# Twelve homes instead of four for the weight tiles of the opening, eight of them in the second half of a work tile

## The chip, the cores and the metric

The kernel is one program on one core of a Trainium2 chip. The core has five engines with instruction streams of their own: TensorE (PE; its weight loads are listed apart as PEld), VectorE (DVE), ScalarE (ACT), GpSimd (POOL) and SyncE (SP), which here only starts transfers. Sixteen DMA engines move data between device memory (HBM) and the on-chip buffer (SBUF). The metric is device time of the whole program in microseconds (us), the median of several runs.

## The reference, cut to what matters

The program is a small transformer on 256 tokens (and 256 context tokens) of width 2048, all in float32: two layers that project, attend and project back, then a mixing block and a gated feed-forward block. What matters here is how the first layer begins:

```
sc, scc = silu(c), silu(c_ctx)
shift, scale, gate       = split(sc  @ w_ada[0] + b_ada[0], 3)     # 2048 x 6144
shift_c, scale_c, gate_c = split(scc @ w_ada[0] + b_ada[0], 3)
h  = rms(x,  norm_w[0]) * (1 + scale)   + shift
hc = rms(xc, norm_w[0]) * (1 + scale_c) + shift_c
u  = h @ w_in[0]          # its columns z (the gate of the output) are computed first
```

So before the first projection can run, two thirds of the first layer's `w_ada` (shift and scale) has to be multiplied with two vectors, and the mean of the squares of x has to be known.

## The kernel before, in words

All weights are cut into tiles of 128 x 1024 float32 (512 KB) and packed by the host in the order of use, as one stream. A planner (`make_plan`) writes the program as a list of steps, and every engine walks the same list and emits its part, so each engine's order is fixed. SP walks the list of loads: it waits until the tile's home (its buffer) is free and starts the transfer. `place_loads` gives out the homes in turn: `RAW` = 4 homes in the buffer `raw` during the opening and most of the program, three more for a while in each layer's attention (`pl.more`: from load a to load b these homes join the turn).

A tile of `w_ada` ("ada chunk", L698) is read by TensorE straight from its home: two k-tiles of 128 rows, against a stationary operand of 32 columns. It is free again once TensorE has done it (semaphore `ada_used`). Eight chunks (group g, c = 0 to 7) make one row of 512 outputs. ScalarE copies the row out (L988, `ada_row`), TensorE turns it into columns (L705, `ada_turn`), VectorE adds the bias (L1342).

A tile of a projection is split: ScalarE copies it rounded into `whi` (L982), VectorE writes the rest into `wlo` (L1332), and the home is free after that (semaphore `lo`). TensorE then does three passes per product (L788 to L790), 24 matmuls of 512 columns per tile in the first projection group, z0 ("z chunk" below).

The opening interleaves these: groups 0 to 7 of `w_ada` (64 chunks), the squares of x (ScalarE squares one of 16 tiles at L994 and L1001, GpSimd adds it to the sum at L1761), their mean (L712, L720), the tiles of h (VectorE L1373, ScalarE L1020 and L1025, VectorE L1384), and five z chunks, one after every few ada chunks. Loads 0 to 70 carry the 64 ada chunks and z chunks 0 to 6. The mean stands in TensorE's order behind ada chunk 2.2 (load 20), z chunk 0 behind chunk 3.1 (load 27), and the last turn (`ada_turn` 7) behind chunk 7.7 (load 70). x itself (4 MB), the constants and the rope table come through GpSimd's queue (q0), everything of SP through q1. GpSimd prepares the rope table (L1770, L1774) ahead of its first sum.

The work tile `T` has 32 rows of 512 numbers per partition. x lies in rows 0 to 15. Rows 16 to 31 are first written when the queries, keys and latents of layer 0 are made, which comes after all of z.

Of the kernel before, what the change touches and what calls it, by code (L numbers as in the profile page):

```python
# [33 lines left out]

CH = 1024
RAW = 4
RAW_ATT = 3
RING = 3
LEAD = 2
# [128 lines left out]
def tail_groups():  # L168
    def span(a):
        return [(a, a + 512)]  # L170

    mix, ffn = [], []
    for g in range(4):
        mix.append(Group("u", None, g, DT, 512, span(512 * g), L + WINDOWS[g], "hn", 4, "w_in_2", "hn_mix" if g == 0 else None))
    for j in range(4):
        mix.append(Group("gc", None, j, DT, 512, span(2 * D + 512 * j), L + 2, "hn", 1, "w_in_2"))
        if j == 0:
            for g in range(4):
                mix.append(Group("ya", None, g, 4, 512, [(0, 512)], L, "pooled", 1, "pool_w_2", "pooled"))
        mix.append(Group("v", None, j, DT, 512, span(3 * D + 512 * j), L + 2, "hn", 1, "w_in_2"))  # L180
        mix.append(Group("gb", None, j, DT, 512, span(D + 512 * j), L, "latent", 4, "w_in_2"))
    for j in range(4):
        mix.append(Group("ga", None, j, DT, 512, span(4 * D + 512 * j), L, "latent", 4, "w_in_2"))
        mix.append(Group("gbr", None, j, DT, 512, span(5 * D + 512 * j), L, "latent", 1, "w_in_2"))
        mix.append(Group("mix", None, j, DT, 512, span(512 * j), L, "conv", 4, "conv_out_w_2",
                         "conv" if j == 0 else None))
    for j in range(4):
        mix.append(Group("wo", None, j, DT, 512, span(512 * j), L, "mixed", 4, "w_o_2", "mixed" if j == 0 else None))
    for g in range(FT // 2):
        ffn.append(Group("ffn", None, g, DT, 512, [(256 * g, 256 * g + 256), (FFN + 256 * g, FFN + 256 * g + 256)], L,  # L190
                         "hn", 2, "w_gate_up_2", "hn_ffn" if g == 0 else None))
    for j in range(4):
        ffn.append(Group("down", None, j, FT, 512, span(512 * j), L, "ffn", 4, "w_down_2", "ffn" if j == 0 else None))
    return mix, ffn
# [15 lines left out]
def slots_of(l):  # L210
    streams = 1 if l else 2
    places = [(u, c, q) for u in range(len(UNITS)) for c in range(streams) for q in range(2)]
    return [Slot(l, s, u, c, q, streams) for s, (u, c, q) in enumerate(places)]
# [7 lines left out]
class Plan:  # L221
# [69 lines left out]
    def place_loads(self):  # L291

        turn, last = list(range(RAW)), {}
        for n in range(len(self.loads)):
# [21 lines left out]
def make_plan():  # L316
    pl = Plan()
    every = []
    layers = [layer_groups(l) for l in range(DEPTH)]
    mix, ffn = tail_groups()  # L320
    for first, second, third in layers:
        every += first + second + third
    every += mix + ffn
    pl.enqueue(every)

    pl.add("start")
    opening = layers[0][0]
    chunks = pl.chunks(opening, DT)
    for i in range(ADA_FIRST):
        for c in range(8):  # L330
            pl.ada(i, c)
            if c == 7:
                pl.add("ada_row", i)
            if i < 2:
                pl.add("square", "x", 8 * i + c)
            if i == 1 and c in (2, 6):
                pl.split()
            if i == 2 and c == 2:
                pl.add("mean", "x")
                pl.add("layer", 0)  # L340
            if c == 3 and i:
                pl.add("ada_turn", i - 1)
                if i % 2 == 0:
                    pl.add("scale", 0, i // 2 - 1)
            if c >= 4 and i and i % 2 == 0:
                pl.add("make", opening[0], 2 * i - 4 + c - 4)
            if i % 2 and i > 1 and (c == 1 or c == 5 and i < 7):
                next(chunks)
    pl.add("ada_turn", ADA_FIRST - 1)
    pl.add("scale", 0, 3)  # L350
    for k in range(12, DT):
        pl.add("make", opening[0], k)
    for _ in chunks:
        pass
    nada, full = [ADA_FIRST * 8], []

    def ada_turn():
        if full:
            pl.add("ada_turn", full.pop())

    def ada_some(n):
        for _ in range(n):
            g, c = divmod(nada[0], 8)
            pl.ada(g, c)
            nada[0] += 1
            if c == 7 and g != ADA_BETWEEN:
                pl.add("ada_row", g)
                full.append(g)

    for l, (first, second, third) in enumerate(layers):  # L370
        if l:
            pl.add("layer", l)
            ada_some(4)
            pl.add("scale", l, None)
            chunks = pl.chunks(first)
            next(chunks)
            pl.add("ada_row", ADA_BETWEEN)
            next(chunks)
            pl.add("ada_turn", ADA_BETWEEN)
            for _ in chunks:  # L380
                pass
        pl.add("rq", l)
        pl.gemm(second)
        pl.flush()
        pl.add("barrier", ("gemm", l))
        pl.left[l] = pl.owner
        pl.turn, pl.owner = 0, {0: None, 4: None}
        slots = slots_of(l)
        att_from = len(pl.loads)
        for s in range(len(slots)):  # L390
            pl.add("score", l, slots, s)
            ada_turn()
            if s < len(ADA_PACE[l]):
                ada_some(ADA_PACE[l][s])
            pl.add("att", l, slots, s)
            if s >= len(slots) - 3:
                pl.add("make", third[0], s - len(slots) + 3)
        more = RAW + RAW_ATT * l
        pl.more.append((att_from, len(pl.loads), list(range(more, more + RAW_ATT))))
        chunks = pl.chunks(third, 3)  # L400
        for s in range(len(slots), len(slots) + 4):
            pl.add("att", l, slots, s)
            next(chunks)
        pl.add("attended", l, slots)
        for _ in chunks:
            pass
        if l == 0:
            for n, p in zip((2, 1, 1, 0), pl.pending):
                pl.add("evac", *p)
                ada_some(n)  # L410
            pl.pending = []
        pl.flush()
    pl.add("tail")
    pl.gemm(mix)
    pl.flush()
    pl.add("ffn")
    pl.gemm(ffn)
    pl.flush()
    pl.add("final")
    pl.place_loads()  # L420
    return pl


def build(nc, d):
    pl = make_plan()
    S = {}

# [5 lines left out]
    hi, lo, used, ada_used = sig("hi"), sig("lo"), sig("used"), sig("ada_used")  # L433
# [41 lines left out]
    place[0] += (WEIGHTS_AT - place[0]) % 256  # L475
    raw = own("raw", [P, RAW, CH])
    whi = own("whi", [P, RING, CH], F32R)
# [14 lines left out]
    T = sb("T", [P, 32, 512], F32, t_at)  # L492
# [106 lines left out]
    def raw_of(n):  # L599

        h = pl.homes[n]
        if h < RAW:
            return raw[:, h, :]
        l, i = divmod(h - RAW, RAW_ATT)
        if i < 2:
            return LF[:, 12 + 2 * i:14 + 2 * i, :].rearrange("p a b -> p (a b)")
        return wlo_f[:, idle_split[l] % RING, :]
# [12 lines left out]
    keys_last = [next(g for g in pl.groups if g.kind == "wkvb" and g.layer == l and g.index == 2) for l in range(DEPTH)]  # L620
# [38 lines left out]
    def sync_engine(SP):  # L659
        SP.dma_start(param[:, :], d["param"]).then_inc(*param_in.up("in"))  # L660
        for n, what in enumerate(pl.loads):
            h = pl.homes[n]
            if pl.before[n] is not None:
                was = pl.loads[pl.before[n]]
                if was[0] == "ada":
                    SP.wait_ge(*ada_used.at(was[1], was[2]))
                else:
                    SP.wait_ge(*lo.at(was[0].id, was[1]))
            elif h >= RAW:
                SP.wait_ge(*used.at("done", keys_last[(h - RAW) // RAW_ATT].id))  # L670
            width = CH
            if what[0] != "ada":
                g, c = what
                width = min(g.kpc, g.kt - c * g.kpc) * g.width
            SP.dma_start(raw_of(n)[:, 0:width], d["stream"][n][:, 0:width]).then_inc(*raw_in[h].up(n))
        for j in range(4):
            SP.wait_ge(*v_ev.at("final", j))
            SP.dma_start(d["out"][:, 4 * j:4 * j + 4, :], SCALED[:, 4 * j:4 * j + 4, :]).then_inc(*out_out[j].up("out"))
        for j in range(4):
            SP.wait_ge(*out_out[j].at("out"))  # L680
# [1378 lines left out]
```

## Time and profile before

| | us |
|---|---|
| median of 3 runs | 3344.04 |
| the three runs | 3344.04, 3333.69, 3369.77 |
| the profiled execution | 3341.04 |
| its span | 3339.7 |
| TensorE busy in the span | 3221.7 (96%) |

The page divides the span into 40 slices of 83.5 us. Its first two slices are the opening and the only ones, beside those around the attention of layer 0, in which TensorE waits much. Windows of the trace give the same for shorter stretches: busy time of each engine, the clock that was granted to TensorE as a share of 2.4 GHz, how busy the 16 DMA engines were and what they moved. The waits say which instruction waited for what, and the timeline says when. Matmul ends are modelled, so the start of the next instruction is the better mark.

### The profile page before, as it was taken

The numbers are of one execution on the slowest core, as the hardware profiler recorded it, in microseconds if no ns is written. First come the engines' busy times: TensorE is split into PE (matmuls) and PEld (weight loads), VectorE is DVE, ScalarE is ACT, GpSimd is POOL, SyncE is SP. The second block draws the span as 40 slices with busy tenths as digits, with TensorE's granted clock in tenths as the row PEclk, the third lists the DMA queues.
The fourth block names the chain that finished last, engine by engine and source line by source line (L and its number), as shares of the span: only waits on it lengthen the run. The fifth ranks groups of instructions, "written<-read, shape, count | busy, mean of one in ns | idle before, by whom it ended". The sixth has DMA issues, their size and how long they took to land.

```text
span 3339.7 us, 52153 instructions
## 1 busy us (share of the span) xinstructions
PE 3221.7 (96%) x21958; PEld 2798.5 (84%) x21958; DVE 1670.4 (50%) x2688; ACT 1360.4 (41%) x2179; POOL 173.5 (5%) x252
## 2 busy tenths in 40 slices
PE   6899999988999999999899999999999999999998
PEld 2488888873558879887559999999999999999998
DVE  1322233376763354354775675556555655555454
ACT  2322232344542254334454443334444444444443
POOL 3001000001001101000111000000000000000000
PEclk9899999998999989999999999999999999999999
DMA  8633222226754246433425455555555555555554
GB/s 305 252 124 123 95 95 95 79 84 252 268 181 153 96 186 209 145 128 106 168 82 197 156 183 184 188 187 192 195 192 195 171 195 194 193 195 194 192 195 158
DMA packets 152826, 566.09 MB, mean 170 GB/s; under 512 B 17520, under 2 KB 17648, under 8 KB 151440
## 3 DMA queue, kind: packets, MB, share of 16 engines
q1 hardware_dynamic: 146160, 529.52, 45.4%
q0 software_dynamic: 6432, 33.23, 2.8%
q8 instruction: 173, 2.83, 0.3%
q14 instruction: 61, 0.50, 0.0%
HBM read 550.10 MB, written 12.58 MB: 168 GB/s over the span
## 4 chain that ended last, share of the span: by engine, by line
PE 91%; DVE 3%; DMA 3%; issue 1%; ACT 1%; POOL 1%; SPq 0%; DVEq 0%; POOLq 0%; ACTq 0%
PE ps L788 20%; PE ps L790 20%; PE ps L789 20%; PE ps L777 7%; PE ps L779 7%; PE ps L778 7%; PE ps L698 3%; DMA sb_raw<-in_stream 2%; PE ps L910 2%; PE ps L873 1%; PE ps L896 1%; PE ps L864 1%; PE ps L889 1%; PE ps L705 1%; DMA sb_rope<-in_rope 1%
## 5 line engine op out<-in xcount | busy, mean ns | idle before, releaser
L1332 DVE TENSOR_TENSOR sb_wlo<-sb_raw,sb_whi 128x1024 fp32r<-128x1024 f32 (+1 forms) x814 | 992.5, 1220 | 1311.2 <-ACT sb_whi L982 1310.0
L982 ACT ACTIVATE sb_whi<-sb_raw 128x1024 fp32r<-128x1024 f32 (+1 forms) x818 | 860.1, 1053 | 1084.1 <-PE ps L790 839.2
L788 PE MATMUL ps<-sb_hn_hi,sb_whi 128*128 128x256 f32 (+4 forms) x2944 | 821.9, 279 | 4.8 <-DVE sb_hn_lo L1404 4.1
L789 PE MATMUL ps<-sb_hn_lo,sb_whi 128*128 128x256 f32 (+4 forms) x2944 | 820.9, 279 | 0.0
L790 PE MATMUL ps<-sb_hn_hi,sb_wlo 128*128 128x256 f32 (+4 forms) x2944 | 820.4, 279 | 0.0
L788 PEld LDWEIGHTS ps<-sb_hn_hi,sb_whi 128*128 128x128 f32 x2944 | 555.6, 189 | 5.6 <-DVE sb_hn_lo L1404 4.4
L790 PEld LDWEIGHTS ps<-sb_hn_hi,sb_wlo 128*128 128x128 f32 x2944 | 556.0, 189 | 0.0
L789 PEld LDWEIGHTS ps<-sb_hn_lo,sb_whi 128*128 128x128 f32 x2944 | 555.6, 189 | 0.0
L779 PE MATMUL ps<-sb_whi,sb_lo 128*128 128x512 f32 (+1 forms) x968 | 375.0, 387 | 0.0
L777 PE MATMUL ps<-sb_whi,sb_hi 128*128 128x512 f32 x896 | 354.8, 396 | 0.0
L778 PE MATMUL ps<-sb_wlo,sb_hi 128*128 128x512 f32 x896 | 349.0, 390 | 0.0
L788 PE MATMUL ps<-sb_hi,sb_whi 128*128 128x512 f32 (+1 forms) x1024 | 343.4, 335 | 0.0
L789 PE MATMUL ps<-sb_lo,sb_whi 128*128 128x512 f32 (+1 forms) x1024 | 341.8, 334 | 0.0
L790 PE MATMUL ps<-sb_hi,sb_wlo 128*128 128x512 f32 (+1 forms) x1024 | 341.8, 334 | 0.0
L788 PEld LDWEIGHTS ps<-sb_hi,sb_whi 128*128 128x128 f32 x1024 | 192.2, 188 | 25.7 <-issue 5.8
L779 PEld LDWEIGHTS ps<-sb_whi,sb_lo 128*128 128x128 f32 x968 | 182.0, 188 | 36.6
L790 PEld LDWEIGHTS ps<-sb_hi,sb_wlo 128*128 128x128 f32 x1024 | 193.3, 189 | 20.0
L789 PEld LDWEIGHTS ps<-sb_lo,sb_whi 128*128 128x128 f32 x1024 | 192.3, 188 | 19.7
L777 PEld LDWEIGHTS ps<-sb_whi,sb_hi 128*128 128x128 f32 x896 | 168.6, 188 | 35.4 <-DVE sb_scr L1373 1.7
L778 PEld LDWEIGHTS ps<-sb_wlo,sb_hi 128*128 128x128 f32 x896 | 168.5, 188 | 34.8
L790 PE MATMUL ps<-sb_ffn_hi,sb_wlo 128*128 128x256 f32 x704 | 194.3, 276 | 0.0
L788 PE MATMUL ps<-sb_ffn_hi,sb_whi 128*128 128x256 f32 x704 | 194.3, 276 | 0.0
(269 smaller groups left out, 4040.5 us busy)
## 6 DMA issues: line engine op xcount, KB each, us to landing
sb_raw<-in_stream SPq DMA_DIRECT2D x943, 512.0 KB, 3.4
sb_lo_f<-in_stream SPq DMA_DIRECT2D x33, 512.0 KB, 6.0
sb_wlo_f<-in_stream SPq DMA_DIRECT2D x16, 512.0 KB, 5.8
sb_raw<-in_stream SPq DMA_DIRECT2D x18, 384.0 KB, 2.9
sb_T<-in_x POOLq DMA_DIRECT2D x1, 4096.0 KB, 18.1
z_scratch<-sb_scr POOLq DMA_DIRECT2D x16, 256.0 KB, 2.6
sb_zb<-z_scratch POOLq DMA_DIRECT2D x16, 256.0 KB, 2.9
sb_bias<-in_bias POOLq DMA_DIRECT2D x4, 1024.0 KB, 8.3
```

The lines of the kernel that those rows point to most:

```text
L698: mm = PE.matmul(PS[t:t + 32, ada_bank(g), :], cond[:, k, :], raw_of(n)[:, 512 * j:512 * j + 512], start=k < 4, stop=k >= 12, tile_positio ...
L705: mm = PE.matmul(PS[:, ada_bank(g), 2 * m:2 * m + 2], arow_of(g)[:, m * P:(m + 1) * P], C("sum4"), start=True, stop=True)
L777: PE.matmul(o, xh[:, xt], wh, start=k == 0, stop=False)
L778: PE.matmul(o, xh[:, xt], wl, start=False, stop=False)
L779: mm = PE.matmul(o, xl[:, xt], wh, start=False, stop=k == g.kt - 1)
L788: PE.matmul(o, whi[:, s, w], xh, start=k == 0, stop=False)
L789: PE.matmul(o, whi[:, s, w], xl, start=False, stop=False)
L790: mm = PE.matmul(o, wlo[:, s, w], xh, start=False, stop=k == g.kt - 1)
L864: PE.matmul(out[h], T[:, T_QN + head, qs], key_nope(head)[:, ks], start=True, stop=True, skip_group_check=True)
L910: mm = PE.transpose(PS[:, 4 + h, kt * P:kt * P + P], p_of(t, h)[:, kt * P:kt * P + P], ident)
L982: AC.activation(whi[:, s, 0:width], raw_of(n)[:, 0:width], ACT.Copy).then_inc(*hi.up((g.id, c)))
L1332: VE.tensor_tensor(wlo[:, s, 0:width], raw_of(n)[:, 0:width], whi[:, s, 0:width].bitcast(F32), ALU.subtract).then_inc(*lo.up((g.id, c)))
```

## The change

The opening's loads get twelve homes: the four of `raw`, and eight in rows 16 to 31 of `T`, two rows each. They join the turn from load 0 up to the load that the planner has reached when the opening's loop ends (load 71, not included). After that four homes are left, as before. The order of the loads, the steps and all computation stay as they are. The homes of the attention stages get other numbers, nothing else.

```diff
+RAW_OPEN = 8
...
             if i % 2 and i > 1 and (c == 1 or c == 5 and i < 7):
                 next(chunks)
+    pl.more.append((0, len(pl.loads), list(range(RAW, RAW + RAW_OPEN))))
...
-        more = RAW + RAW_ATT * l
+        more = (RAW + RAW_OPEN) + RAW_ATT * l
...
         if h < RAW:
             return raw[:, h, :]
-        l, i = divmod(h - RAW, RAW_ATT)
+        if h < RAW + RAW_OPEN:
+            a = 16 + 2 * (h - RAW)
+            return T[:, a:a + 2, :].rearrange("p a b -> p (a b)")
+        l, i = divmod(h - (RAW + RAW_OPEN), RAW_ATT)
...
-            elif h >= RAW:
-                SP.wait_ge(*used.at("done", keys_last[(h - RAW) // RAW_ATT].id))
+            elif h >= (RAW + RAW_OPEN):
+                SP.wait_ge(*used.at("done", keys_last[(h - (RAW + RAW_OPEN)) // RAW_ATT].id))
```

SP's order of loads at the start of the program, before (`ada_used` is TensorE's release of a home, `lo` VectorE's):

```order
L660 DMA sb_param<-in_param 128x364 [waits barrier_Pool_Activation_PE_DVE_SP_release]
L675 DMA sb_raw<-in_stream 128x1024 x4
L675 DMA sb_raw<-in_stream 128x1024 [waits ada_used] x11
L675 DMA sb_raw<-in_stream 128x1024 [waits lo]
L675 DMA sb_raw<-in_stream 128x1024 [waits ada_used] x4
L675 DMA sb_raw<-in_stream 128x1024 [waits lo]
```

and with the change:

```order
L665 DMA sb_param<-in_param 128x364 [waits barrier_Pool_Activation_PE_DVE_SP_release]
L680 DMA sb_raw<-in_stream 128x1024 x4
L680 DMA sb_T<-in_stream 128x1024 x8
L680 DMA sb_raw<-in_stream 128x1024 [waits ada_used] x4
L680 DMA sb_T<-in_stream 128x1024 [waits ada_used] x7
L680 DMA sb_T<-in_stream 128x1024 [waits lo]
```

Before, the fifth load waits for a release; now the thirteenth is the first that does. Load 15 waited for the split of z chunk 0 (load 11); now load 23 does.

ScalarE's order in the same place, before (the squares are L1001, the splits L982, the copy of a row L988):

```order
L1001 ACTIVATE sb_scr<-sb_T 128x512 [waits p_ev] x4
L988 ACTIVATE sb_scr<-ps 128x512 [waits ada_used]
L1001 ACTIVATE sb_scr<-sb_T 128x512 [waits p_ev] x4
L982 ACTIVATE sb_whi<-sb_raw 128x1024 [waits raw_in3]
L1001 ACTIVATE sb_scr<-sb_T 128x512 [waits p_ev] x4
L982 ACTIVATE sb_whi<-sb_raw 128x1024 [waits raw_in0]
L988 ACTIVATE sb_scr<-ps 128x512 [waits e_ev,ada_used]
```

and with the change:

```order
L1006 ACTIVATE sb_scr<-sb_T 128x512 [waits p_ev] x4
L993 ACTIVATE sb_scr<-ps 128x512 [waits ada_used]
L1006 ACTIVATE sb_scr<-sb_T 128x512 [waits p_ev] x4
L987 ACTIVATE sb_whi<-sb_T 128x1024 [waits raw_in11]
L1006 ACTIVATE sb_scr<-sb_T 128x512 [waits p_ev] x4
L987 ACTIVATE sb_whi<-sb_T 128x1024 [waits raw_in4]
L993 ACTIVATE sb_scr<-ps 128x512 [waits e_ev,ada_used]
```

The order is the same. The two splits and the row copies stand between the squares as they did, and wait for tiles that have other homes.

## Rows read from the trace of the kernel before

**Rows 1.** The page: TensorE's busy tenths in 40 slices of the span.

```profile
PE   6899999988999999999899999999999999999998
```

**Rows 2.** Windows: us, busy time by engine, granted clock, DMA share, GB/s.

```profile
0.00:10.00 10.00, 1.92 (x4) 0.19 (x4) 0.66 (x9) 1.52 (x2) 2.48 (x8) 1.00 0.85 318
10.00:15.00 5.00, 0.00 (x0) 0.00 (x0) 0.00 (x0) 0.00 (x0) 0.00 (x0) 1.00 1.04 445
15.00:20.00 5.00, 1.92 (x4) 0.19 (x4) 0.00 (x0) 0.00 (x0) 0.00 (x0) 1.00 0.90 375
20.00:22.70 2.70, 1.92 (x4) 0.19 (x4) 0.00 (x0) 1.67 (x3) 0.00 (x0) 1.00 1.04 423
...
56.00:147.00 91.00, 77.80 (x360) 36.57 (x359) 27.10 (x61) 26.59 (x48) 0.00 (x0) 0.87 0.80 294
147.00:160.00 13.00, 13.00 (x61) 10.89 (x62) 8.83 (x18) 8.72 (x15) 0.00 (x0) 1.00 0.29 96
```

**Rows 3.** Waits of SP, 0 to 160 us: total us, times, longest.

```profile
SPq L675 <- PE ps L698: 97.3, 49, 11.1
SPq L675 <- DVE sb_wlo L1332: 32.9, 9, 11.3
```

**Rows 4.** Timeline, 16 to 60 us: start, length, what, idle before.

```profile
16.07 1.92 PE L698 MATMUL ps<-sb_raw,sb_cond 128*32 128x512 f32 x4 [9.52 <-DMA sb_raw<-in_stream]
20.20 0.63 ACT L994 ACTIVATE sb_scr<-sb_T 128x512 f32<-128x512 f32 x1 [16.78 <-DMA sb_T<-in_x]
22.83 2.48 POOL L1770 TENSOR_TENSOR sb_rope<-sb_rope,sb_const 128x512 f32<-128x512 f32 x2 [19.77 <-DMA sb_rope<-in_rope]
27.26 20.38 POOL L1761 TENSOR_TENSOR sb_scr<-sb_scr 128x512 f32<-128x512 f32 x14
45.74 1.92 PE L698 MATMUL ps<-sb_raw,sb_cond 128*32 128x512 f32 x4 [4.53 <-DMA sb_raw<-in_stream]
52.50 1.26 POOL L1761 TENSOR_TENSOR sb_scr<-sb_scr 128x512 f32<-128x512 f32 x1 [4.85 <-ACT sb_scr L1001]
55.17 1.05 PE L712 MATMUL ps<-sb_const,sb_scr 128*128 128x1 f32 x8
57.88 1.05 PE L698 MATMUL ps<-sb_raw,sb_cond 128*32 128x512 f32 x4
```

**Rows 5.** DMA of 14 to 17 us by queue: packets, MB, share.

```profile
q0 software_dynamic: 35, 1.08, 83.4%
q1 hardware_dynamic: 40, 0.14, 11.4%
```

**Rows 6.** Timeline, 60 to 105 us: tiles of h, z chunk 0, ada chunks, turns.

```profile
63.08 0.69 DVE L1384 TENSOR_TENSOR sb_lo<-sb_scr,sb_hi 128x512 fp32r<-128x512 f32 x1 [0.84 <-ACT sb_hi L1025]
67.80 0.50 PE L788 MATMUL ps<-sb_hi,sb_whi 128*128 128x512 f32 x1
73.47 1.06 PE L698 MATMUL ps<-sb_raw,sb_cond 128*32 128x512 f32 x8
74.46 1.05 PE L705 MATMUL ps<-sb_const,sb_scr 128*128 128x2 f32 x8
75.44 1.06 PE L698 MATMUL ps<-sb_raw,sb_cond 128*32 128x512 f32 x8
90.02 1.92 PE L698 MATMUL ps<-sb_raw,sb_cond 128*32 128x512 f32 x4 [2.43 <-DMA sb_raw<-in_stream]
93.67 3.64 PE L698 MATMUL ps<-sb_raw,sb_cond 128*32 128x512 f32 x16
```

**Rows 7.** Timeline, 146 to 148 us: the last row and turn.

```profile
146.29 0.60 ACT L988 ACTIVATE sb_scr<-ps 128x512 f32<-128x512 f32 x1 [11.37 <-PE ps L698]
146.94 1.05 PE L705 MATMUL ps<-sb_const,sb_scr 128*128 128x2 f32 x8 [0.69 <-ACT sb_scr L988]
```

**Rows 8.** Windows with several loads queued; the second in layer 0's attention.

```profile
33.00:38.00 5.00, 3.03 (x15) 0.57 (x11) 0.00 (x0) 2.79 (x5) 4.57 (x4) 1.00 0.99 333
770.00:780.00 10.00, 5.66 (x36) 1.10 (x24) 5.08 (x18) 6.53 (x19) 0.12 (x1) 0.84 0.98 371
```

## The prediction

> **What bounds the kernel now.** I read the page's slices first: TensorE is busy in nine tenths or more of nearly every slice, and the first is an exception, at six tenths [rows 1]. The change touches loads 0 to 70, so I cut the opening into windows. From 56 to 147 us TensorE is busy 77.8 of 91.0 us at a mean granted clock of 0.87, and the DMA engines are at 0.80 and move 294 GB/s; in the 13 us behind it TensorE is busy throughout at clock 1.00 and the DMA engines at 0.29 [rows 2]. So the opening is short of weights until its last turn starts at 146.94 us [rows 7], and from there TensorE is the bound. The waits of SP say why the weights are late: of the opening it spends 97.3 us waiting for TensorE to release a home and 32.9 us for VectorE to finish a split [rows 3]. Loads are issued late while the engines that carry them have room. What is won ahead of 146.94 us is kept whole, because nothing behind it waits for an absolute time.
>
> **The first part: up to the mean.** Nothing of the computation changes. The sixteen squares need x and GpSimd. x is in at 20.20 us, and GpSimd starts on the rope table at 22.83, sums from 27.26 on, and has done 14 sums in 20.38 us [rows 4], 1.41 us each with one gap. The fifteenth sum starts only at 52.50, after 4.85 us of waiting for ScalarE, whose square stands behind a split and a row copy that wait for late tiles. The mean follows at 55.17 behind ada chunks that are late too [rows 4]. With the tiles early, the fifteenth sum ends at 27.26 + 15 x 1.41 = 48.4; the two splits and the row copies still stand between the squares, for which I add 1.1. Call it 49.5 us.
>
> Are the tiles early? By 22.7 us the windows give 3.18 + 2.23 + 1.88 + 1.14 = 8.4 MB [rows 2]. 5.5 MB of that are x, constants, parameters and rope table, so 2.9 MB or 5.6 tiles of 0.524 MB are weights. For the pitch behind it the trace has stretches in which several loads are queued: 371 GB/s at share 0.98 with seven homes in the attention, 333 at 0.99 with four homes here [rows 8], and 423 at the end of the table's load [rows 2]. That is 1.41, 1.57 and 1.24 us per tile. I take 1.38, nearest to the row with the most homes, and keep 1.24 and 1.57 as ends. Load n then lands at 22.7 + (n + 1 - 5.6) x 1.38: load 20, the last ahead of the mean, at 44, before the sums are done. The mean starts at 49.5 instead of 55.2. This is worth **5.7 us**.
>
> Does x come later, with twelve weight loads beside it instead of four? From 14 to 17 us q0 moved 1.08 MB and q1 0.14 [rows 5], though loads 1 to 3 were queued on q1 at that time (TensorE got the first of them only at 16.07 us [rows 4]). x had nearly nine tenths of the bytes against a waiting weight queue. A longer queue waits just as much; I cost this at 0, with a rival below.
>
> **The second part: from the mean to the last turn.** Before it is 146.94 - 55.17 = 91.8 us. TensorE's own work in it, at the full level of its clock:
> - mean and rows until ada chunk 2.3: 57.88 - 55.17 = 2.7 [rows 4];
> - 45 ada chunks. Two that lie ready take 74.46 - 73.47 = 0.99 together [rows 6], while one that arrives alone takes 0.98 or more. 45 x 0.49 = 22.1;
> - 6 turns x (75.44 - 74.46) = 5.9 [rows 6];
> - 5 z chunks x (73.47 - 67.80) = 28.3 [rows 6];
> - row copy ahead of the last turn 146.94 - 146.29 = 0.7 [rows 7].
>
> Sum 59.7 us. Three more terms:
> - Tiles of h. The first is ready 3.9 us behind turn 1's end (63.77 against 59.85) [rows 6]. TensorE needs about 3 us for the six ada chunks between. So z chunks 0, 2 and 4, the first of each pair of fresh tiles, wait 0.3, 1.0 and 0.9: 2.2 us.
> - The clock. TensorE stands still from 45 to 49.5. In this trace the wait of 4.5 us ahead of 45.74 is followed by chunks of 1.92 us, and the one of 2.4 us ahead of 90.02 too; at 93.67 four chunks take 3.64 instead of 2.0 [rows 4, 6]. The mean clock of 0.87 [rows 2] is what such stretches leave; they last 8 to 12 us. I let everything from the mean to z chunk 0 run at the 1.2 GHz level. This costs 6.7 us: a second time the mean and rows (1.9), the lone chunk 2.3 (1.4), the turn (0.8) and six chunks (2.6).
> - DMA. z chunk 0 starts at 63.5. Until then TensorE has released all homes up to load 27, so SP has issued up to 39, and load 39 lands at 70: the queue does not run dry by more than 1 us. Load 45 lands at 78, needed at 85. Load 63 lands at 103, needed at 107. Load 70 lands at 113, needed at 117. Each is early, so 0. At 1.57 us load 70 lands at 125.4.
>
> Last turn: 49.5 + 59.7 + 2.2 + 6.7 = **118.1 us**, against 146.94: 28.8 earlier. For further falls of the clock, of which the stretch before has three and each costs up to 4 us when TensorE is the bound, I take back 2. From load 71 on four homes are back; their last users (ada chunks 6.6 to 7.1) are long done, and a z chunk needs a tile in 5.7 us, so the stage behind is as before: 0. The attention homes have new numbers only: 0. Eight more semaphores: 0.
>
> Sum: 3341.0 - 28.8 + 2 = 3314.2 against the profiled execution. The median of the runs shown is 3.0 above it, and I give the result as **3316**.
>
> The Trainium skill, "DMA: Bandwidth & Descriptors", Specifications, puts the HBM limit of one core at about 358 GB/s, which speaks against more homes being of full use. By it, as an estimate, a tile takes 1.46 us, load 70 lands at 118 and the last turn starts near 121, 3 us later than in my sum. The trace exceeds it in short windows and is near it in the long one.
>
> **The rivals.**
> 1. *The stream is slower than I take it* (as at 33 to 38 us, 333 GB/s at share 0.99 [rows 8]). Load 70 lands at 125.4, the turn starts at about 128, and the gain is 19: 3325. For it: this row is of this very stage. Against it: it has four homes, and 371 comes with seven. Chance 0.17.
> 2. *More than 1%.* No fall of the clock while TensorE waits for the mean, and 1.24 us per tile. The turn starts at 118.1 - 6.2 = 112, as z chunk 0 is then held by its tile of h. The gain is 35: 3309 or less. For it: the windows at 423 and 445 GB/s [rows 2]. Against it: 4.5 us of waiting brought the low clock before. Chance 0.18.
> 3. *x comes later.* If q0 and q1 share evenly, x and rope table (5.3 MB) need twice their bytes at 0.38 MB/us, until about 28.6 us instead of 22.8, and the mean starts at 55.3. The rest is TensorE's and follows: gain 23, 3321. Chance 0.06.
> 4. *Slower: x starves behind twelve queued tiles.* The place is q0 in the first 30 us. If x got a fifth of the bytes, it and the table would take 5.3 / 0.076 = 70 us, the mean would start at 97, and the last turn at 165: 18 us later, 3362. It decides from a mean at 79 us on (147 less the 68 that follow it). Rows 5 speak against it. The chance of a result that is slower is 0.03, and over 1% slower (33 us) needs x later still: 0.01.
> 5. *The change does nothing*, because the sums and tiles of h are the chain anyway: 3344. Against it: the ladder above leaves that chain 28 us of room. Chance 0.04.
>
> My forecast, a gain of 23 to 33 us by the sum above, has 0.52.
>
> **How the numbers follow.** The low end is rival 2's (3309) less 5 for the scatter of the runs (3334 to 3370), 3304. The high end is rival 1's with 10 for the scatter above, 3336. One per cent is 33 us, about what a measurement of this kernel tells from no change. Faster by over 1% is rival 2 and a little scatter, 0.20; slower by over 1% 0.01 and scatter, 0.02; within it 0.78.
>
> The Trainium skill, "TensorE: Matmul & The Clock Gate", HAM oscillation, says that matmul groups which wait for their data fall back to the half clock each time, so feeding them early gives back more than the waits. By that rule the mean clock from 56 us to the last turn should rise above the 0.87 of rows 2; I have it rise, but for the one fall at the mean.
>
> **What would show it.** SP's waits for L698 shift by eight loads, and twelve loads stand open. x lands at 20 to 21 us. The mean starts at 49 to 51. The waits of L698 for tiles behind it are below 5 us in all. The last turn starts at 116 to 122. DMA moves 340 to 400 GB/s from 23 to 60 us. Behind the last turn all stages have their old lengths. I am wrong if x lands after 25 us, if DMA stays below 330 GB/s with loads queued, or if a stage behind grows by what the opening lost.

## The result

The changed kernel takes 3313.09 us (median of 4 runs, 3312.15 to 3315.54), the kernel before 3343.49 (4 runs, 3333.69 to 3369.77). The ratio is 0.989 with a 95% interval from 0.984 to 0.993, so it is faster by about 1.1%. Forecast were 3316 us and a range from 3304 to 3336. The span of the profiled execution fell from 3339.7 to 3310.8 us.

The windows of the changed kernel, cut as in [rows 2] but with the long one behind 56 us ending at 118 us, 2 us behind its own last turn (columns: window and length; busy time of PE, PEld, DVE, ACT, POOL; granted clock; DMA share; GB/s):

```profile
20.00:22.70 2.70, 1.94 (x6) 0.18 (x4) 0.00 (x0) 1.67 (x3) 0.00 (x0) 1.00 1.03 419
22.70:30.00 7.30, 6.21 (x24) 0.99 (x24) 0.00 (x0) 0.63 (x1) 6.56 (x6) 1.00 1.02 410
30.00:40.00 10.00, 8.04 (x34) 2.49 (x32) 0.00 (x0) 5.59 (x9) 9.00 (x8) 0.79 1.03 410
40.00:50.00 10.00, 5.13 (x18) 0.65 (x16) 4.57 (x4) 5.89 (x9) 9.14 (x7) 0.84 1.02 409
50.00:60.00 10.00, 9.26 (x52) 5.40 (x52) 3.01 (x10) 1.18 (x4) 0.12 (x1) 0.68 1.01 392
56.00:118.00 62.00, 58.53 (x359) 34.54 (x358) 26.94 (x65) 26.03 (x47) 0.00 (x0) 1.00 0.95 371
118.00:131.00 13.00, 13.00 (x59) 10.76 (x58) 9.16 (x15) 8.91 (x15) 0.00 (x0) 1.00 0.23 67
```

From 20 to 50 us the DMA engines are full and carry 409 to 419 GB/s. From 56 us on they carry 371 where they carried 294 before, and TensorE is busy 58.5 of 62 us at clock 1.00, where it was 77.8 of 91 at 0.87.

The timeline of the same execution at the places of [rows 4] and [rows 7] (start, length, instruction, idle time before it):

```profile
20.41 0.63 ACT L999 ACTIVATE sb_scr<-sb_T 128x512 f32<-128x512 f32 x1 [16.85 <-DMA sb_T<-in_x]
23.05 2.49 POOL L1775 TENSOR_TENSOR sb_rope<-sb_rope,sb_const 128x512 f32<-128x512 f32 x2 [19.98 <-DMA sb_rope<-in_rope]
27.49 22.64 POOL L1766 TENSOR_TENSOR sb_scr<-sb_scr 128x512 f32<-128x512 f32 x15
50.17 1.87 PE L717 MATMUL ps<-sb_const,sb_scr 128*128 128x1 f32 x8 [4.42 <-POOL sb_scr L1766]
54.62 1.89 PE L703 MATMUL ps<-sb_T,sb_cond 128*32 128x512 f32 x4
56.44 1.05 PE L710 MATMUL ps<-sb_const,sb_scr 128*128 128x2 f32 x8
...
115.94 1.05 PE L710 MATMUL ps<-sb_const,sb_scr 128*128 128x2 f32 x8 [0.74 <-ACT sb_scr L993]
```

x is in 0.2 us later than before. GpSimd now does its 15 sums without a long stop, and TensorE waits for them, no longer for tiles. The mean starts at 50.17 us instead of 55.17, the last turn at 115.94 instead of 146.94: 31.0 us, of which 5.0 lie ahead of the mean and 26.0 behind it.

Less than half of the 26.0 us is time in which TensorE stood still for a tile. These are the ada chunks from the mean to the last turn (busy us, mean ns of one matmul, idle time before them), the first line of the kernel before, the others of the changed one:

```profile
L698 PE MATMUL ps<-sb_raw,sb_cond 128*32 128x512 f32 x182 | 41.9, 732 | 11.9 <-DMA sb_raw<-in_stream 11.9
```

```profile
L703 PE MATMUL ps<-sb_T,sb_cond 128*32 128x512 f32 x120 | 16.8, 615 | 0.0
L703 PE MATMUL ps<-sb_raw,sb_cond 128*32 128x512 f32 x60 | 9.0, 596 | 0.2 <-DMA sb_raw<-in_stream 0.2
```

The wait went from 11.9 to 0.2 us, and the same chunks took 25.8 us instead of 41.9. Both sides of that are in the prediction's rows: at the low level of the clock a lone chunk takes 1.92 us, and two that lie ready take 0.99 together at the full one, where a lone one takes nearly as much by itself [rows 4, 6]. How the 16 us divide between the two was not measured.

Behind the last turn the work is as it was. Two windows of equal length, the first of the kernel before from 1.1 us behind its last turn, the second of the changed one from 3.1 us behind its own:

```profile
148.00:3339.70 3191.70, 3115.27 (x21502) 2755.90 (x21502) 1639.10 (x2614) 1318.28 (x2108) 147.07 (x225) 0.98 0.47 163
```

```profile
119.00:3310.80 3191.80, 3116.13 (x21494) 2758.10 (x21492) 1637.57 (x2607) 1318.14 (x2107) 147.17 (x225) 0.98 0.48 163
```

From the last turn to the end of the span it was 3192.8 us before and is 3194.9 now, 2.1 us more. In nine of the twelve profiled executions of this document that stretch lies between 3190.4 and 3195.3, so the 2.1 us are no more than its scatter. Of the 31.0 us of the opening 28.9 arrived at the end. In the experiments below I compare the start of the last turn rather than spans, because the late stages scatter by more than some of these kernels differ (last section).

### The profile page after: what moved, and what is told of

Read it like the earlier page. It is cut to its first block, busy times and chain, and to the rows that moved or that the text cites. A ratio compares the mean times of both kernels' runs of the same rounds, so it can differ in the third digit from the quotient of the medians.

```text
span 3310.8 us, 52153 instructions
## 1 busy us (share of the span) xinstructions
PE 3206.1 (97%) x21958; PEld 2801.9 (85%) x21958; DVE 1671.6 (50%) x2688; ACT 1360.2 (41%) x2179; POOL 174.5 (5%) x252
## 4 chain that ended last, share of the span: by engine, by line
PE 92%; DVE 3%; DMA 2%; issue 1%; ACT 1%; POOL 1%; SPq 0%; POOLq 0%; DVEq 0%; ACTq 0%
PE ps L793 20%; PE ps L795 20%; PE ps L794 20%; PE ps L782 7%; PE ps L784 7%; PE ps L783 7%; PE ps L703 2%; PE ps L915 2%; PE ps L878 1%; PE ps L901 1%; DMA sb_raw<-in_stream 1%; PE ps L869 1%; PE ps L894 1%; PE ps L710 1%; POOL sb_scr L1766 1%
## 5 line engine op out<-in xcount | busy, mean ns | idle before, releaser
L987 ACT ACTIVATE sb_whi<-sb_raw 128x1024 fp32r<-128x1024 f32 x812 | 853.6, 1052 | 1068.6 <-PE ps L795 841.7
```

What stands on the lines that cost most here:

```text
L987: AC.activation(whi[:, s, 0:width], raw_of(n)[:, 0:width], ACT.Copy).then_inc(*hi.up((g.id, c)))
```

## The experiments

All are the changed kernel with one edit, but for e7. "Last turn" is the start of the eighth L710 (L705 in the kernels with four homes). The times are those of one profiled execution each. x landed between 18.97 and 20.41 us in them (29.14 in e6), and differences of 1 us in the table are within that scatter: the change and e8 are the same kernel. The last column comes from all runs of each.

| kernel | mean starts | last turn | between | ratio to before (95%) |
|---|---|---|---|---|
| four homes (before) | 55.17 | 146.94 | 91.8 | 1 |
| six, e5 | 51.59 | 129.81 | 78.2 | 0.993 (0.990 to 0.995) |
| eight, e3 | 49.83 | 121.67 | 71.8 | 0.994 (0.991 to 0.997) |
| twelve, the change | 50.17 | 115.94 | 65.8 | 0.989 (0.984 to 0.993) |
| twelve, e8 | 48.93 | 115.09 | 66.2 | 0.990 (0.987 to 0.992) |
| twelve from load 21 on, e1 | 54.21 | 122.03 | 67.8 | 0.993 (0.990 to 0.995) |
| twelve up to load 20, e2 | 48.70 | 143.41 | 94.7 | 1.000 (0.997 to 1.004) |
| twelve, x in 4 KB rows, e6 | 58.84 | 124.44 | 65.6 | 0.993 (0.990 to 0.997) |
| four, rope table later, e7 | 51.07 | 147.91 | 96.8 | 0.999 (0.996 to 1.002) |
| twelve, rope table later, e4 | 44.56 | 111.38 | 66.8 | 0.989 (0.985 to 0.993) |
| the same, e10 | 45.41 | 111.29 | 65.9 | 0.988 (0.984 to 0.992) |
| twelve, filler ahead of the mean, e9 | 49.57 | 114.49 | 64.9 | 0.992 (0.989 to 0.996) |

**Which part of the opening needs the homes.**

```diff
-    pl.more.append((0, len(pl.loads), list(range(RAW, RAW + RAW_OPEN))))
+    pl.more.append((21, len(pl.loads), list(range(RAW, RAW + RAW_OPEN))))    # e1
+    pl.more.append((0, 21, list(range(RAW, RAW + RAW_OPEN))))                # e2
```

> The eight extra homes join only at load 21, the first tile behind the mean; up to it four homes as before. My theory (two separate gains: about 5 us ahead of the mean, the rest because TensorE finds its tiles ready behind it): the mean starts at 55 us as in the kernel before, the DMA engines then run at about 400 GB/s, and the last turn starts at 118 to 121 us, 26 to 29 us ahead of the kernel before. Rival (the lead has to be built up while TensorE waits for the squares, so that late homes are worth little): last turn at 130 us or later.

> The extra homes are there for loads 0 to 20 only. My theory: the mean starts at 50 us as with the change, but behind it the stretch costs what it cost before (91 us, less 0 to 3 us), so the last turn starts at 139 to 142 us, 5 to 8 us ahead of the kernel before. Rival (the lead is what counts): last turn at 130 us or earlier.

Late homes alone start the last turn at 122.03, 24.9 us ahead of before (1 us later than I expected). Early homes alone give 3.5 us, less than expected, and no change of the time that can be measured. The windows show what the DMA engines did. First e1, then e2:

```profile
56.00:100.00 44.00, 42.27 (x233) 23.44 (x234) 18.90 (x41) 17.45 (x31) 0.00 (x0) 1.00 1.02 405
```

```profile
50.00:56.00 6.00, 5.43 (x27) 3.58 (x31) 0.87 (x3) 0.26 (x1) 0.00 (x0) 0.62 0.04 8
56.00:100.00 44.00, 35.65 (x162) 16.34 (x155) 16.83 (x37) 16.49 (x30) 0.00 (x0) 0.92 0.85 296
```

With late homes the DMA engines are full. In e2 they stand still from 50 to 56 us (share 0.04): the four homes are full while TensorE waits for the mean, and behind it the stream starts afresh at 296 GB/s. Between the mean and the last turn TensorE waited 14.8 us for tiles in e2 and 11.9 in the kernel before. The two parts do not add: the early one is worth 6.1 us beside the late one (122.03 - 115.94) and 3.5 without it.

**How many homes.**

```diff
-RAW_OPEN = 8
+RAW_OPEN = 4    # e3: eight homes
+RAW_OPEN = 2    # e5: six homes
```

> Eight homes instead of twelve (four of them in the work tile). By the count of loads that may stand open: the mean at 50 us as with the change; the bursts of ten and twelve ada chunks behind z chunks 1 and 3 outrun the queue by 1 to 2 us each. Last turn at 117 to 120 us, 27 to 30 us ahead of the kernel before. Rival (a tile in flight takes long with a long queue, so each home counts): halfway between four and twelve, about 131 us.

> Six homes (two of them in the work tile). From the mean to the last turn the stretch took 91.8 us with four homes, 71.8 with eight, 65.8 with twelve. My theory (what counts is whether the lead covers a burst of ten or twelve ada chunks): the first two homes bring more than the next two; mean at 51 to 52 us, then about 79 us, last turn at 128 to 133. Rival (linear in the homes between four and eight): 134 to 135 us.

Two more homes bring 17.1 us, the next two 8.1, the last four 5.7. e5 came out as expected. e3 is 1.7 us behind the expected range, but far from the rival's 131. From the mean to the last turn TensorE waited 11.9 us for tiles with four homes, 7.1 with six, 4.7 with eight (nearly all of it in the bursts of ten and twelve ada chunks) and 0.2 with twelve; what is left at twelve is TensorE's own work and 2.5 us of waiting for tiles of h.

**What protects x.** The change puts twelve tiles beside x.

```diff
-                PO.dma_start(T[:, 0:16, :], d["x"]).then_inc(*x_in.up("in"))
+                for k in range(0, 16, 2):
+                    PO.dma_start(T[:, k:k + 2, :], d["x"][:, k:k + 2, :]).then_inc(*x_in.up("in"))
```

> Twelve homes, and x comes as eight transfers with rows of 4 KB instead of one with rows of 32 KB. My theory (x had nearly nine tenths of the bytes because its pieces are eight times as long as those of the weights, and the length of the weight queue did not matter): both queues share evenly, x is in at 24 to 26 us and the rope table at 27 to 29 instead of 20.4 and 23.1, the mean starts at 55 us and the last turn at 119 to 122. Rival (a queue's turn does not depend on the size of its pieces): x at 20 to 21 us, last turn at 116. Rival (x waits for the twelve tiles): mean at 66 us or later.

The DMA queues from 14 to 17 us (packets, MB, share of the 16 engines), with the change, and in e6:

```profile
q0 software_dynamic: 34, 1.11, 86.5%
q1 hardware_dynamic: 33, 0.12, 9.7%
```

```profile
q1 hardware_dynamic: 173, 0.63, 52.1%
q0 software_dynamic: 171, 0.62, 51.2%
```

In both, the two queues move nearly equal numbers of packets: 34 and 33, 171 and 173 (with four homes 35 and 40 [rows 5]). What differs is the size. x's packets carried 33 KB each and the weights' 4 KB; in e6 all carry 4 KB. By this x keeps nine tenths of the bytes against twelve tiles (q0 had 1.08 MB against four [rows 5]) and falls to half when its rows are cut. x came in at 29.14 us in e6, the mean started at 58.84, both later than I expected (24 to 26, 55). The likely reason is that q0 carries the constants, x and the table, and shares from the first microsecond, which I had not counted; no run separates it. The last turn was 8.5 us later than with the change, nearly all of the mean's 8.7. The Trainium skill, "DMA: Bandwidth & Descriptors", Queues, rings and completion order, says that each DMA engine goes round its queues packet by packet; the counts of this trace agree.

**What bounds the mean.**

```diff
                 PO.wait_ge(*const_in.at("in"))
                 make_rope(0)          # taken out of the step "start", ahead of the sums
...
+            elif st[0] == "mean":     # and put behind them
+                PO.wait_ge(*const_in.at("in"))
+                make_rope(0)
```

> Twelve homes, and GpSimd prepares the rope table behind the sums of the squares instead of ahead of them. My theory (with twelve homes the mean is bound by GpSimd's sums, not by tiles): sums start at about 21 instead of 27.5 us, the mean at 44 to 45 us instead of 50.2, just behind load 20 at 42 to 43; the last turn at 109 to 111 us, where load 70 becomes the bound (22.7 + 65.4 x 1.28 = 106.4, and 3.5 behind it): 5 to 7 us less than with the change alone. Rival (the wait is hidden by the tiles of h or by the weight stream): no change, 116 us.

> e4 again with more rounds, beside a kernel with the same homes: last turn at 110 to 112 us, median 3303 to 3308, 0.987 to 0.989 of the kernel before.

> Four homes as before, and the rope table is prepared behind the sums. With twelve homes this brought 4.6 us. My theory (with four homes too the squares hold up the split of z chunk 0, and so home 3 and load 15): load 15 is issued 5 us earlier, the mean starts at 50 to 51 instead of 55.2, the last turn at 142 to 143. Rival (with four homes the tiles alone set the mean): 146 to 147 us, as before.

With twelve homes the mean moves from 50.2 to 44.6 and the last turn to 111.4, 4.6 us, a little less than expected. Counted from the landing of x, the mean came 29.7 us later in the change, e2, e3, e6, e8 and e9, and 25.3 in e4 and e10: in these kernels it follows GpSimd. The DMA engines are at 1.03 and 409 GB/s in e4 from 56 to 100 us, and in the longer bursts of ada chunks TensorE is paced by the tiles, one every 1.28 us:

```profile
56.00:100.00 44.00, 42.90 (x246) 23.57 (x244) 15.54 (x36) 15.42 (x28) 0.00 (x0) 1.00 1.03 409
```

```profile
74.48 1.05 PE L703 MATMUL ps<-sb_T,sb_cond 128*32 128x512 f32 x4 [0.23 <-DMA sb_T<-in_stream]
75.76 1.05 PE L703 MATMUL ps<-sb_T,sb_cond 128*32 128x512 f32 x4 [0.23 <-DMA sb_T<-in_stream]
77.04 1.05 PE L703 MATMUL ps<-sb_T,sb_cond 128*32 128x512 f32 x4 [0.23 <-DMA sb_T<-in_stream]
```

TensorE is busy 42.9 of 44 us in the same window, and its last four chunks find their tiles ready, so both are near their limit.

With four homes (e7) the same edit moves the mean by 4.1 us, as my theory said, and the last turn not at all (147.91, where I expected 142 to 143). The rival's number came out, though for another reason than its own: not the tiles ahead of the mean, but the stream behind it, for whose tiles TensorE then waited 16.4 us instead of 11.9. The median of e4 was 3304.95 us in 6 runs, that of e10 3311.57 in 11, above the expected 3303 to 3308. Ratios of 0.989 and 0.988 beside 0.989 and 0.990 for the change do not tell the version from it; the profiles do, by 4 us. By its last turn it is the earliest of these kernels.

**The clock at the mean.**

```diff
             elif st[0] == "mean":
+                PE.wait_ge(*const_in.at("in"))
+                for _ in range(4):
+                    PE.matmul(PS[:, 4, :], ident, const[:, 0:512], start=True, stop=True)
                 PE.wait_ge(*p_ev.at("sq", "x", DT - 1))
```

> Twelve homes, and between ada chunk 2.2 and the mean TensorE does four matmuls of constants into a bank that nothing uses yet (about 0.9 us each at the full clock), so that it stands still for 1 to 2 us there instead of 4.4. My theory (the 4.4 us of standing still bring the 1.2 GHz level, which costs 2.5 us from the mean to turn 1 and passes whole to the end): the mean at 50 to 51 us, from its start to turn 1 3.7 us instead of 6.3, last turn 2 to 3 us earlier, 113 to 114 us. Rival (the tiles of h or the weight stream bind behind it anyway, or the clock falls all the same): 115 to 117 us.

TensorE in e9 around the mean (L717):

```profile
45.10 3.70 PE L934 MATMUL ps<-sb_const 128*128 128x512 f32 x8
49.57 1.05 PE L717 MATMUL ps<-sb_const,sb_scr 128*128 128x1 f32 x8 [0.78 <-POOL sb_scr L1768]
51.19 1.16 PE L725 MATMUL ps<-sb_const,sb_ssq 128*128 128x128 f32 x8 [0.57 <-DVE sb_ssq L1357]
52.28 1.84 PE L703 MATMUL ps<-sb_T,sb_cond 128*32 128x512 f32 x4
54.05 1.87 PE L710 MATMUL ps<-sb_const,sb_scr 128*128 128x2 f32 x8
55.85 1.93 PE L703 MATMUL ps<-sb_T,sb_cond 128*32 128x512 f32 x8
```

The mean ran at the full level, but the low one came all the same, from 52.3 us on, with no wait over 0.8 us in the 7 us ahead of it. From the mean to turn 1 it took 4.5 us instead of 6.3, where I expected 3.7, and the last turn came at 114.49, 0.6 us ahead of e8 and 1.5 ahead of the change. x had landed at 19.84, 19.20 and 20.41 us in the three, so this shows no clear gain at the last turn. The theory that the wait of 4.4 us brings the low level does not hold as I put it. e10 has the same fall, from about 47.0 to 50.7 us, with a wait of 0.6 us.

Over all profiled executions, the five in which TensorE waited 1.8 us or more right ahead of the mean (the change, e2, e3, e6, e8) had the low level behind it and took 5.3 to 6.3 us from the mean to turn 1. Of the seven others, five took 3.7 us and two had the low level: e9 (4.5) and e10 (5.3, while e4, the same kernel, took 3.7). So the low level came with every such wait, but also twice without one. What brings it about there is open.

**The control.**

> The changed kernel again, on the chip and in the hour of these runs: last turn at 115 to 117 us, median 3311 to 3316.

Last turn 115.09, median 3311.06: as expected.

## Why the prediction was right, point by point

- **The bound, and that the gain is kept.** Right but for 2.1 us. Up to the last turn SP waited for TensorE 36.6 us instead of 97.3 [rows 3], and 28.9 of the 31.0 us arrived at the end. Its waits for VectorE hardly changed, 25.8 us after 20.9. SP's waits from 0 to 116 us:

```profile
SPq L680 <- PE ps L703: 36.6, 27, 5.4
SPq L680 <- DVE sb_wlo L1337: 25.8, 4, 9.2
```

- **The mean.** 49.5 forecast, 50.17 measured; 15 sums took 22.64 us, 1.51 each instead of 1.41 with 1.1 added, and x was 0.2 us late. The 1.41 is not what [rows 4] give over all 14 sums, which is 20.38 / 14 = 1.46; with that the forecast would have been 50.2. But the term of 5.7 us was put down as if it stood by itself. e2 and e7 show that with four homes behind the mean it is worth 3.5 us or nothing: the stream behind the mean takes it back.
- **x.** 0 was right, and e6 shows what it rests on. Rivals 3 and 4 fell.
- **The tile pitch.** This size was off: 1.38 us taken, 1.28 measured (0.524 MB at 410 GB/s), near the end of 1.24. The row nearest to the true value was that of the end of the table's load [rows 2]; the row at 770 us [rows 8], which I took as nearest because it has the most homes, was too slow. The error cost nothing, since with twelve homes TensorE binds; in e4, where tiles pace the longer bursts, the last turn came at 111.4, near the 109.9 that the new pitch gives. Rival 1 fell with it. The HBM limit of 358 GB/s that the Trainium skill gives ("DMA: Bandwidth & Descriptors", Specifications) did not hold here: 409 and 410 GB/s stood for 27 us.
- **From the mean to the last turn.** 68.6 us by my sum, 65.8 measured. The clock was mis-sized: I let everything up to z chunk 0 run at 1.2 GHz, at a cost of 6.7 us. The low level ended with chunk 2.3, and from the mean to turn 1 it took 6.3 us where the kernel before took 3.7, so the cost was 2.6 us. No further fall came: the mean granted clock was 1.00 from 56 to 118 us. So the 2 us taken back for further falls were not due; that the stretch behind the last turn took 2.1 us more made up for them by luck. That the wait at the mean is the cause of the low level, as the term supposed, is not shown: e9 had that level without a wait over 0.8 us. The tiles of h cost 2.5 us where I had 2.2, but with another division: z chunks 0 and 2 waited 1.3 and 1.2 us and z chunk 4 not at all, where I had 0.3, 1.0 and 0.9.
- **The queue not running dry.** Nearly: SP issued nothing from 61.5 to 67.9 us. Load 40 needs the home of load 28, whose split ScalarE starts only at 65.60 us, behind four tiles of h and a row copy; VectorE ends its part at 67.91. SP's timeline from 60 to 70 us:

```profile
59.84 1.65 SPq L680 DMA_DIRECT2D sb_raw<-in_stream  x3
67.93 1.28 SPq L680 DMA_DIRECT2D sb_T<-in_stream  x3
```

  The DMA share was 0.83 to 0.86 from 68 to 80 us behind it. I counted TensorE's releases only, and overlooked this one; the stock of tiles covered it.
- **Rival 2** (over 1%) had one of its two conditions, the pitch, and not the other. The ratio came out between it and the forecast: I gave 0.20 to a gain of over 1%, and the measured 1.1% has an interval from 0.7 to 1.6.
- **The sum and the signs.** The sum was 3314.2 us for the profiled execution, which took 3312.15. With the 3.0 us added for the median it makes 3317.2 and not the 3316 that I gave. Of the signs named, two were missed: the last turn came at 115.94, just ahead of 116 to 122, and DMA moved 409 and 410 GB/s from 23 to 50 us, above 340 to 400.

## What to carry to other kernels

In this kernel the homes had to cover the longest burst of chunks that are used up quickly, not the mean rate: four homes left the DMA engines at 0.80 while TensorE waited, and each pair more brought less (17, 8, then 3 us). Tiles that come early gave back more than the waits for them, since the chunks themselves took 16 us less. Memory that is written only later in the program is a free place for them. Before moving a producer earlier, ask what stands behind it: with four homes 4 us at the mean were worth nothing, with twelve 4.6.

## What the runs showed of the hardware

- Queues shared the DMA engines by packets, so the size of a transfer's rows set its share: 86.5% of the engines' time with 32 KB rows, 51.2% with 4 KB rows.
- Nearly all of the larger scatter between runs of one kernel may have one source. In the profiled executions of e3 and e10 TensorE did 2550 matmuls from 2700 to 3000 us, in all others 2649 or 2650, fully busy and with a granted clock of 1.00 in both. e2 has the slower pace for a part: 342 matmuls in each 40 us from 2300 to 2500 us, where the change has 356, also at clock 1.00. Matmul of e10, then of e4, which is the same kernel:

```profile
2600.00:3300.00 700.00, 700.00 (x5946) 1.00 0.56 187
```

```profile
2600.00:3300.00 700.00, 694.20 (x6121) 1.00 0.57 189
```

  e10's span is 3333.8 us and e4's 3304.0, with last turns at 111.29 and 111.38. A matmul of 256 columns came every 117.6 ns instead of 113.2, 4% more, and the clock's rows don't show it. What sets it is open.
